# A down projection with tokens on the output partitions

## What is computed

```python
def rmsnorm(x, g):
    y = x * rsqrt(mean(x * x, axis=-1, keepdims=True) + 1e-6)
    return y * g

def conv_gated_mlp(h, w_gate, w_up, conv_ffn_w, conv_ffn_b, w_down):
    g = causal_dwconv(h @ w_gate, conv_ffn_w, conv_ffn_b)     # 2048 -> 6144
    return (gelu(g) * (h @ w_up)) @ w_down                    # 6144 -> 2048

x = x + rmsnorm(hybrid_mixer(rmsnorm(x, norm_mix_pre), ...), norm_mix_post)   # called x1 below
h = rmsnorm(x, norm_ffn_pre)
x = x + rmsnorm(conv_gated_mlp(h, ...), norm_ffn_post)
```

## Time and profile before

| | |
|---|---|
| median of 3 runs | 2304.57 us (2303.58 to 2305.54) |
| the profiled execution | 2304.29 us |
| its span, first to last instruction | 2302.6 us |
| TensorE matmul, busy | 2230.5 us, 97% |
| VectorE, ScalarE, busy | 1559.4 us, 989.0 us |
| mean granted TensorE clock | 0.985 of full speed |
| last matmul of the down projection starts | 2263.23 us |

### The profile page before, as it was taken

How to read it: one execution, slowest core, us unless ns; L and a number is a source line. 1 busy time by engine, 2 the same in 40 slices (tenths; PEclk the granted TensorE clock), 3 DMA queues, 4 the chain that set the end, 5 groups by cost and what they waited for, 6 DMA issues and landing times.

```text
span 2302.6 us, 34618 instructions
## 1 busy us (share of the span) xinstructions
PE 2230.5 (97%) x13324; PEld 1970.7 (86%) x13324; DVE 1559.4 (68%) x2022; ACT 989.0 (43%) x1232; POOL 202.0 (9%) x250
## 2 busy tenths in 40 slices
PE   8999999999899899999999999999999999999993
PEld 6788888888688688999999999999998888888882
DVE  8776667767755677788888888888885454544543
ACT  5444545544422354444444444444443343333431
POOL 3000000003300000111111111111102000000002
PEclk9899999999999999999999999999999999999997
DMA  4222222222242335877777777777767322222224
GB/s 170 68 93 79 90 93 82 93 85 75 95 141 91 114 128 163 216 206 199 206 205 202 199 202 205 204 204 203 207 175 284 125 93 99 93 99 91 100 91 82
DMA packets 94966, 325.15 MB, mean 141 GB/s; under 512 B 10753, under 2 KB 14977, under 8 KB 94737
## 3 DMA queue, kind: packets, MB, share of 16 engines
q1 hardware_dynamic: 68160, 237.18, 30.2%
q0 software_dynamic: 24400, 82.36, 16.9%
q10 hardware_dynamic: 2304, 4.20, 0.5%
HBM read 302.69 MB, written 21.00 MB: 141 GB/s over the span
## 4 chain that ended last, share of the span: by engine, by line
PE 93%; DVE 2%; issue 1%; ACT 1%; POOL 1%; DMA 1%; SPq 0%; DVEq 0%; POOLq 0%; ACTq 0%
PE bank L1447 31%; PE bank L1449 31%; PE bank L1448 30%; PE bank L1509 1%; POOL out L476 1%; DVE acc_b L1102 1%; DMA x_sb<-xT 0%; ACT act_hi L612 0%; DVE w_lo L842 0%; PE bank L1477 0%; DMA h_t<-h_spill 0%; ACT w_hi L486 0%; DVE rms L863 0%; PE bank L1528 0%; ACT act_hi L636 0%
## 5 line engine op out<-in xcount | busy, mean ns | idle before, releaser
L1447 PE MATMUL bank<-act_hi,w_hi 128*128 128x512 f32 (+1 forms) x2880 | 1026.7, 356 | 22.3 <-DVE act_lo L857 13.5
L1449 PE MATMUL bank<-act_hi,w_lo 128*128 128x512 f32 (+1 forms) x2880 | 1019.0, 354 | 0.0
L1448 PE MATMUL bank<-act_lo,w_hi 128*128 128x512 f32 (+1 forms) x2880 | 1013.7, 352 | 0.0
L1447 PEld LDWEIGHTS bank<-act_hi,w_hi 128*128 128x128 f32 x2880 | 545.3, 189 | 103.0 <-DVE w_lo L842 10.9
L1449 PEld LDWEIGHTS bank<-act_hi,w_lo 128*128 128x128 f32 x2880 | 544.9, 189 | 81.1
L1448 PEld LDWEIGHTS bank<-act_lo,w_hi 128*128 128x128 f32 x2880 | 544.9, 189 | 78.2 <-issue 0.7
L1449 PE MATMUL bank<-tsum,w_lo 128*128 128x256 f32 x1344 | 374.1, 278 | 0.0
L1448 PE MATMUL bank<-tsum,w_hi 128*128 128x256 f32 x1344 | 374.1, 278 | 0.0
L1447 PE MATMUL bank<-tsum,w_hi 128*128 128x256 f32 x1344 | 374.0, 278 | 0.0
L852 DVE TENSOR_TENSOR w_lo<-raw,w_hi 128x1024 fp32r<-128x1024 f32 x96 | 117.6, 1225 | 271.1 <-ACT w_hi L492 271.1
L842 DVE TENSOR_TENSOR w_lo<-raw,w_hi 128x1024 fp32r<-128x1024 f32 x138 | 171.9, 1246 | 185.7 <-ACT w_hi L486 183.5
(11 more groups left out here) (222 smaller groups left out, 1811.4 us busy)
## 6 DMA issues: line engine op xcount, KB each, us to landing
raw<-weights SPq DMA_DIRECT2D x318, 512.0 KB, 3.5
raw_s<-weights SPq DMA_DIRECT2D x84, 512.0 KB, 5.0
raw_s<-weights POOLq DMA_DIRECT2D x84, 512.0 KB, 6.1
raw_a<-weights SPq DMA_DIRECT2D x42, 512.0 KB, 5.2
h_spill<-h_out POOLq DMA_DIRECT2D x48, 256.0 KB, 3.7
h_t<-h_spill POOLq DMA_DIRECT2D x24, 512.0 KB, 6.5
x<-xT POOLq DMA_DIRECT2D x16, 256.0 KB, 2.9
out<-x ACTq DMA_DIRECT2D x16, 256.0 KB, 2.1
```

Source lines behind the costliest of these rows:

```text
L1447: pe.matmul(dst, ah, bh, start=start, stop=False, skip_group_check=goes_on)
L1448: pe.matmul(dst, ah, bl, start=False, stop=False, skip_group_check=goes_on)
L1449: return pe.matmul(dst, al, bh, start=False, stop=stop, skip_group_check=goes_on)
```

## The change

The operands of the down projection trade places: the stationary one is a hidden tile's 128 tokens, the moving one 512 output channels of the weights. A bank then holds 128 tokens by 512 channels, and a group gives the same 512 channels as before for all tokens, in four banks of 128 tokens each. From this follows the rest:

- Groups 0 to 2 are copied out of PSUM by VectorE (`tensor_copy`) into `y_tile(i)`, 128 tokens by 2048 channels, and ScalarE squares them with a row sum (`accum_out`) into `y_sq`. The multiplications by `rms` and by the gain and the additions into `acc` are gone.
- The factor `rms` cancels in the norm but for its epsilon, so the norm's epsilon becomes one per token, `eps_y`. It is computed once, in the gate projection: four more matmuls (`column_sum`) in `x1_sum`, one small VectorE instruction, and a wait of TensorE before unit `U_FF+12`.
- In the last unit, for each 128 tokens: ScalarE squares the bank with a row sum, VectorE adds the four sums, ScalarE takes the root of 128x1, VectorE the reciprocal, ScalarE scales the last 512 channels out of PSUM, VectorE the first 1536.
- TensorE transposes the result back, 16 tiles of four 128x128 transposes, through four banks, in the order `LIFTS`. Twelve tiles are taken by VectorE, which multiplies by the gain and adds x1 in one instruction, and SyncE stores them two at a time with plain DMAs. The other four (tiles 0 to 3, `ADDED`) are taken by ScalarE into two buffers, and GpSimd stores them with adding DMAs; tiles 2 and 3 wait until the stores of tiles 0 and 1 have landed.
- x1 for the twelve tiles is read back from `out` (3 MB, one DMA of GpSimd) into `x1_b`, where the first hidden tiles lay, in the last group.

```diff
+ADDED = 4
+LIFTS = (4, 5, 0, 6, 7, 1, 8, 9, 2, 10, 11, 3, 12, 13, 14, 15)
...
+        def h_tokens(t, s, kt, i):
+            c = HS + i % 2 * P
+            return t[:, 4 * s + 2 * kt + i // 2, c:c + P]
...
+            for k in range(0, KT - ADDED, 2):
+                sp.wait_ge(taken, k + 2)
+                sp.dma_start(out[:, ADDED + k:ADDED + k + 2], x1_b[:, k:k + 2]).then_inc(stored, 16)
+            sp.wait_ge(stored, 16 * (KT - ADDED) // 2)
...
             pool.wait_ge(x1_stored, 16 * KT)
-            for k in range(KT):
-                pool.wait_ge(yd_scaled, k + 1)
-                pool.dma_start(out[:, k], yd_tile(k), accum_op=ALU.add).then_inc(stored, 16)
-            pool.wait_ge(stored, 16 * KT)
+            pool.wait_ge(h_split, 3 * PER_GROUP + 6)
+            pool.dma_start(x1_b[:], out[:, ADDED:KT]).then_inc(x1_back_landed, 16)
+            for k in range(ADDED):
+                pool.wait_ge(added, k + 1)
+                pool.dma_start(out[:, k], y_out[:, k % 2], accum_op=ALU.add).then_inc(y_added[k % 2], 16)
+            for e in range(2):
+                pool.wait_ge(y_added[e], 16 * ADDED // 2)
...
             def down_square(g, i):
-                act.wait_ge(wd_taken, 4 * g + i + 1)
-                act.activation(sq[:, 0], sq[:, 1], ACT.Square).then_inc(wdsq_done, 1)
+                if g < GROUPS - 1:
+                    act.wait_ge(wd_taken, QT * g + i + 1)
+                    src = y_tile(i)[:, S * g:S * g + S]
+                else:
+                    act.wait_ge(last_done, i + 1)
+                    src = DOWN_BANKS[g % 2][i][:]
+                act.activation(sq[:, 0], src, ACT.Square, accum_out=y_sq[:, i, g:g + 1]).then_inc(wdsq_done, 1)
...
-            for i in range(4):
-                act.wait_ge(wd_scaled, i + 1)
-                act.activation(sq_last[:, i], yd_tile(KT - 4 + i), ACT.Square).then_inc(wdsq_done, 1)
-            root(6, SUM, std)
+            for i in range(QT):
+                down_square(GROUPS - 1, i)
+                act.wait_ge(y_summed, i + 1)
+                act.activation(y_r[:, 1, i:i + 1], y_r[:, 0, i:i + 1], ACT.Sqrt, scale=1.0 / D,
+                               bias=eps_y[:, i:i + 1]).then_inc(y_std_done, 1)
+                act.wait_ge(y_r_done, i + 1)
+                act.activation(y_tile(i)[:, 3 * S:], DOWN_BANKS[1][i][:], ACT.Copy, scale=y_r[:, 2, i:i + 1]).then_inc(
+                    y_scaled_a, 1)
+            for n, k in enumerate(LIFTS):
+                if k < ADDED:
+                    act.wait_ge(lifted, n + 1)
+                    if k > 1:
+                        act.wait_ge(y_added[k % 2], 16 * (k // 2))
+                    act.activation(y_out[:, k % 2], LIFT[n % 4][:], ACT.Copy, scale=col("g_ffn_post", k)).then_inc(
+                        added, 1)
...
             invert_root(5, rms[:], std, 4)
+            dve.wait_ge(sum_done, 6)
+            dve.tensor_scalar(eps_y[:], PT[2][:, 0:QT], EPS / D, EPS * EPS, ALU.mult, ALU.add).then_inc(eps_y_done, 1)
             chain(dve.memset(gb[:, 0:2], 0.0))
             split(U_FF + 12, 0)
...
             def down_tile(g, i):
-                t = 4 * g + i
-                if i:
-                    add_down_square(t - 1)
-                else:
+                if not i:
                     dve.wait_ge(unit_used, U_HID + (g + 1) * PER_GROUP)
-                dve.tensor_tensor(sq[:, 1], DOWN_BANKS[g % 2][i][:], rms[:], ALU.mult).then_inc(wd_taken, 1)
-                dve.wait_ge(wd_taken, t + 1)
-                dve.tensor_scalar(yd_tile(t), sq[:, 1], col("g_ffn_post", t), None, ALU.mult)
+                dve.tensor_copy(y_tile(i)[:, S * g:S * g + S], DOWN_BANKS[g % 2][i][:]).then_inc(wd_taken, 1)
...
-            for i in range(4):
-                dve.wait_ge(last_done, i + 1)
-                dve.tensor_tensor(yd_tile(KT - 4 + i), DOWN_BANKS[1][i][:], rms[:], ALU.mult).then_inc(wd_scaled, 1)
-                if i:
-                    add_down_square(KT - 4 + i - 1)
-            invert_root(6, rms[:], std, 5)
-
-            dve.wait_ge(wd_scaled, 4)
-            for k in range(KT):
-                if k < KT - 4:
-                    dve.tensor_tensor(yd_tile(k), yd_tile(k), rms[:], ALU.mult).then_inc(yd_scaled, 1)
-                else:
-                    dve.scalar_tensor_tensor(out=yd_tile(k), in0=yd_tile(k), scalar=col("g_ffn_post", k), in1=rms[:],
-                                             op0=ALU.mult, op1=ALU.mult).then_inc(yd_scaled, 1)
+            for i in range(QT):
+                dve.wait_ge(wdsq_done, QT * (GROUPS - 1) + i + 1)
+                dve.tensor_reduce(y_r[:, 0, i:i + 1], y_sq[:, i], AXX, ALU.add).then_inc(y_summed, 1)
+                dve.wait_ge(y_std_done, i + 1)
+                dve.reciprocal(y_r[:, 2, i:i + 1], y_r[:, 1, i:i + 1]).then_inc(y_r_done, 1)
+                dve.wait_ge(y_r_done, i + 1)
+                dve.tensor_scalar(y_tile(i)[:, 0:3 * S], y_tile(i)[:, 0:3 * S], y_r[:, 2, i:i + 1], None,
+                                  ALU.mult).then_inc(y_scaled_d, 1)
+            dve.wait_ge(x1_back_landed, 16)
+            for n, k in enumerate(LIFTS):
+                if k >= ADDED:
+                    dve.wait_ge(lifted, n + 1)
+                    dve.scalar_tensor_tensor(out=x1_b[:, k - ADDED], in0=LIFT[n % 4][:], scalar=col("g_ffn_post", k),
+                                             in1=x1_b[:, k - ADDED], op0=ALU.mult, op1=ALU.add).then_inc(taken, 1)
...
                 channel_sum(SB[2], acc[:])
+                column_sum(PT[2], acc)
...
             tile(U_FF + 10, PJ[1], between=x1_sum)
+            pe.wait_ge(eps_y_done, 1)
             tile(U_FF + 12, PT[2])
...
                 for kt in range(2):
+                    w = slice(S * kt, S * kt + S)
                     for i, bank in enumerate(out_banks):
-                        last = product(halves(bank[:]), w_tile(s, 4 * kt + i),
-                                       (h_half(act_hi, s, kt), h_half(act_lo, s, kt)),
-                                       start and kt == 0, stop and kt == 1)
+                        last = product(bank[:], (h_tokens(act_hi, s, kt, i), h_tokens(act_lo, s, kt, i)),
+                                       (w_hi[:, s, w], w_lo[:, s, w]), start and kt == 0, stop and kt == 1)
...
-            pe.wait_ge(wdsum_ready, 1)
-            pe.matmul(SUM[:], ones[:], acc[:], start=True, stop=False)
-            pe.wait_ge(wdsq_done, KT)
-            pe.matmul(SUM[:], ones[:], sq_last[:, 3], start=False, stop=True).then_inc(sum_done, 1)
+            for n, k in enumerate(LIFTS):
+                if n >= 4:
+                    before = LIFTS[:n - 3]
+                    at_least(pe, taken, sum(b >= ADDED for b in before))
+                    at_least(pe, added, sum(b < ADDED for b in before))
+                if k == 12:
+                    pe.wait_ge(y_scaled_a, QT)
+                for i in range(QT):
+                    if n == 0:
+                        pe.wait_ge(y_scaled_d, i + 1)
+                    last = pe.transpose(LIFT[n % 4][:, P * i:P * i + P], y_tile(i)[:, P * k:P * k + P], ident[:])
+                last.then_inc(lifted, 1)
```

More of the change, by code:

```diff
@@ L150, in block_kernel @@
         cols = sb("cols", [2, QT])
+        eps_y = sb("eps_y", [QT])
+        y_sq = sb("y_sq", [QT, GROUPS])
+        y_r = sb("y_r", [3, QT])
         banks = [ctx.enter_context(nc.psum_tensor(f"bank{i}", [P, S], F32)) for i in range(8)]
@@ L153, in block_kernel @@
         DOWN_BANKS = (banks[0:4], banks[4:8])
-        SUM = banks[0]
+        LIFT = banks[0:4]
         region_a = ExitStack()
@@ L162, in block_kernel @@
         sb("act_hi_first", [KT // 2, S])
-        yd_a = sb("yd_a", [KT // 2, S])
+        y_a = sb("y_a", [2, D])
         sb("act_lo_first", [KT // 2, S])
-        yd_b = sb("yd_b", [KT // 2, S])
+        y_b = sb("y_b", [2, D])
         mix = ExitStack()
@@ L237, in block_kernel @@
         h_t = sb_in(hid, "h_t", [FT, S])
-        sq_last = sb_in(hid, "sq_last", [4, S])
+        y_out = sb_in(hid, "y_out", [2, S])
         hid.close()
+        fin = ExitStack()
+        x1_b = sb_in(fin, "x1_b", [KT - ADDED, S])
+        fin.close()
         names = """par_landed hi_done split_done unit_used consts_set zeros_set
@@ L252, in block_kernel @@
             a11_landed a12_landed a22_landed s3_half s3_landed s2_done s4_done
-            p1_copied pu_done pw_done c22_done c11_taken c12_done c12_taken c21_done wd_scaled last_done
-            wd_taken wdsq_done wdsum_ready diag_done spread_done yd_scaled
+            p1_copied pu_done pw_done c22_done c11_taken c12_done c12_taken c21_done last_done
+            wd_taken wdsq_done y_summed y_std_done y_r_done y_scaled_a y_scaled_d diag_done spread_done eps_y_done
+            x1_back_landed lifted added taken
             stored dve_chain""".split()
@@ L268, in block_kernel @@
          a11_landed, a12_landed, a22_landed, s3_half, s3_landed, s2_done, s4_done,
```

(21 more changed lines are left out.)

5 lines of the change are left out of this document (removed).

## The result

The changed kernel takes 2337.91 us at the median (2336.42 to 2338.63), the kernel before 2305.06 on the same chip: a ratio of 1.0142, with a 95% interval of 1.0125 to 1.016. It is 33 us slower, where 10.6 us less were forecast.

A forecast was written before the change was run, and what follows sets the result against it. TensorE bounds the down projection, so the gain had to come from the 39.0 us end, bound by DMA engines while stores run. End at 2291.0 plus 1.0 gives 2292.0 against 2302.6, -10.6 us: forecast 2294.0, range 2288 to 2301.

The forecast's parts named there:

- The matmuls: Down projection: moving operand as one run of 512 in place of two of 256, 0.2286 us either way, cost nothing.
- Rival (c): Down projection: traded operands raise matmul pitch; gain gone at +4.6 ns, slower at +6.6 ns, time 2309.2 us; chance 0.06.
- The column sums: Gate projection: four fp32 matmuls in TensorE's queue cost their whole length, +1.0 us, bounds 0.5 and 1.3.
- Reading x1 back: Last group: 3.1 MB beside the weight loads costs nothing; if a load were held up, a stall of 3.2 us, once.
- No ScalarE wait: Last group: a sign expected in the profile after, that ScalarE does not wait for a weight load.
- The norm: Last unit: four rounds of 2.15 us, one table load of 1.28, scaling done 6.1 us behind the last matmul.
- The clock of the lifts: End: TensorE's transposes back run at half clock, 0.86 us a tile, the last at 2283.1.
- rival (a): End: full clock for the lifts, 0.44 us a tile, time 2291.0 us; chance 0.18.
- The stores: End: DMA work of 14.4 us against 24.7, a lone adding store landing in 4.0, closing 5.0, end at 2291.0.
- rival (b): End: stores share DMA engines badly, tiles 2 and 3 wait for 0 and 1; time 2301.0 at 8 us landings; chance 0.15.

The follow-up runs named there:

- the experiment with the pad alone: Kernel before, with 160 unused bytes a partition allocated behind cols and nothing else changed: 2348.11 us, ratio 1.0187.
- one pair of kernels: Kernel before and changed kernel, each with eps and cols (changed: also its three small tensors) ahead of raw, distance 0: 2324.23 and 2313.61 us.
- the other: Kernel before with 64 bytes ahead of w_hi2, 2289.61 us; changed kernel with that, small tensors away and hidden halves 64 bytes lower, 2273.06 us.

## Why the prediction was wrong

**The matmuls: wrong, and decisive.** The step that failed is "0.2286 us either way. Cost nothing." That put the change of the matmuls' pitch at nothing; the runs show +44 us from the shifted tensors and +10 from the traded operands. The step had compared the form of the moving operand (one run or two) in the earlier trace rows, and left out where the operands lie: both stages had the distance 64, so the rows could not show it. Two parts of the change move that. The three small tensors shift everything behind them by 160 bytes, which costs 44 us over the whole kernel (2348.11 - 2304.46 in the experiment with the pad alone). And trading places turns the distance of 64 in the down projection into -64, which costs 10 us by itself. With the small tensors in the way too, the two don't add: the distance there is then -224, or 32, which is on the same slow level. I had also taken the rest of the kernel as untouched because its code was; a tensor's size is part of the code of every stage.

**Rival (c)** had the right sign, the right place and nearly the price for one part (+4.4 ns, 10.2 us, where it said +4.6 for a lost gain), with the wrong reason: other engines' writes. It got 0.06. That the forecast is wrong if the pitch moves stood among its signs, but the pitch was looked for in the down projection alone.

**The column sums: right.** Forecast +1.0 us. TensorE in the changed kernel:

```profile
858.86 0.95 PE L1514 MATMUL bank<-ones,acc 128*128 128x1 f32 x8
859.67 0.48 PE L1478 MATMUL bank<-act_hi,w_hi 128*128 128x512 f32 x1
```

From 858.86 to 859.67 they hold the queue, for 0.81 us.

**Reading x1 back: right in cost, wrong in cover.** TensorE never stood still for it, but it took 12.8 us to land, and the weight load beside it 9.4, where I had 7.5 at most against a slack of 8.5. ScalarE waited for that load. The chain of waits of the changed kernel (us in total, times, longest), and the window of that stretch:

```profile
ACT w_hi L516 <- DMA raw<-weights: 4.4, 1, 4.4
```

```profile
2200.00:2220.00 20.00, 20.00 (x88) 16.05 (x87) 7.22 (x7) 7.26 (x8) 0.55 (x1) 1.00 0.68 260
```

TensorE is busy for 20.00 of 20.00 us all the same. The splits start every 5.60 us (2201.97, 2207.57), and the one that waited for the load starts at 2213.96, only 0.8 us behind that beat: for the rest of the 4.4 us it would have waited for TensorE to free the slot. "No ScalarE wait" was the wrong sign to look for.

**The norm: right.** Round 1's square starts 2.02 us ahead of round 2's (forecast 2.15), one table load, and the last scaling ends 5.4 us after the last matmul (forecast 6.1). The row sum ended at 2304.86, the table load started at 2304.88 and the root at 2306.17, so this trace has no room for the drain that the Trainium skill (ScalarE: Activation LUTs, What ACT_TABLE_LOAD costs) puts beside a load.

**The clock of the lifts: half right.** The windows of the changed kernel; the column behind POOL is the clock, then DMA share and GB/s:

```profile
2308.00:2312.00 4.00, 0.97 (x5) 0.36 (x3) 2.68 (x6) 3.12 (x8) 0.00 (x0) 1.00 0.00 0
...
2314.00:2316.00 2.00, 2.00 (x10) 2.00 (x11) 1.50 (x2) 0.00 (x0) 0.00 (x0) 0.50 0.03 8
...
2317.00:2318.00 1.00, 1.00 (x10) 1.00 (x9) 1.00 (x2) 0.00 (x0) 0.91 (x1) 0.87 1.00 406
2318.00:2320.00 2.00, 2.00 (x20) 2.00 (x19) 1.88 (x4) 0.69 (x1) 0.89 (x1) 1.00 0.87 108
```

The clock fell after nearly idle microseconds, as forecast, and the first transposes ran at 0.50: two start every 0.43 us, 0.86 for a tile. But from about 2317 it was back at full speed, with nothing but transposes on TensorE since 2313.82. Its timeline on both sides of that point:

```profile
2315.80 0.63 PE L1785 MATMUL bank<-ident,y_a 128*128 128x128 f32 x2
2316.22 0.64 PE L1785 MATMUL bank<-ident,y_b 128*128 128x128 f32 x2
...
2318.04 0.38 PE L1785 MATMUL bank<-ident,y_b 128*128 128x128 f32 x2
2318.26 0.38 PE L1785 MATMUL bank<-ident,y_a 128*128 128x128 f32 x2
```

Two in 0.22 us are 0.44 for a tile, the price of rival (a), 0.18. The forecast held for the first 3 us and rival (a) for the rest. What the Trainium skill says of transposes and the clock (TensorE: Matmul & The Clock Gate, PE-mode transpose), and by which the half clock would have lasted to the end, doesn't hold in this trace: the clock rose from 0.50 to 1.00 under transposes alone.

**The stores: right in total.** The DMA queues of the changed kernel from 2313 to 2336, 23 us, and the landings of the adding stores (line 499):

```profile
q1 hardware_dynamic: 864, 3.15, 34.5%
q0 software_dynamic: 576, 1.05, 31.0%
```

```profile
DMA to landing us min/median/max: 4.2/6.2/7.4
```

65.5% of 23 us are 15.1 us of all engines, where 14.4 were forecast. The landings took longer than the 4.0 that I gave them, and ScalarE waited 2.6 and 3.3 us for the buffers of tiles 2 and 3 (the brackets in the first section's timeline). This is rival (b)'s wait, there but small, and four buffers, which take it away, gained nothing that the runs can tell. The early return of the clock and the longer landings worked against each other: 28.4 us from the last matmul's end, with 27.4 forecast. That the total came so near is in part luck.

So the sum of what the change computes was right in size: at equal distances it is worth 10.6 us by one pair of kernels and 11.5 by the other. The sum lacked a term of +44 for where the tensors lie, which doesn't belong to anything that the change computes.

## What to carry to other kernels

A few bytes of new tensors shift every operand that is allocated behind them, and swapping the operands of a matmul turns the sign of their distance. Here the first cost four times what the edit gained, and the second about all of it. Busy time and clock show none of it: take the starts of two matmuls, or their count in a window, in a stage that the diff doesn't touch, and compare them before looking for a cause in the new code. When two versions are compared, pad them so that the operands have the same distances; then try the distance itself. Here 64 bytes in one place were worth 0.6% to the old kernel, and two such places 1.3% to the changed one (2302.72 to 2273.06): distance 0 modulo 256 bytes for 512 columns, 64 to either side for this kernel's 256-column stage. Work out the distance with its sign, from the addresses of both.

## What the runs showed of the hardware that I had not expected

- The pitch of a stream of fp32r matmuls whose operands start at multiples of 32 bytes depends on the moving operand's start less the stationary one's, modulo 256 bytes. With 512 columns: 0.2267 us at 0, 0.2292 at +64, 0.2333 to 0.2344 at the other multiples of 32, -64 among them. With 256 columns, in the kernels: 0.1133 at 64 and at -64, 0.1196 to 0.1200 at 0, 0.1184 at 224.
- At distance 0 with both operands 16 or 4 bytes off a multiple of 32 it was 0.2333 and 0.2375 with 512 columns.
- The same offsets gave 0.114 or 0.118 us with 256 columns in two kernels; what else decides stayed open.
- The granted clock went from 0.50 (2316 to 2317) to 1.00 (2318 to 2320) while TensorE did nothing but transposes.
- A table load stood between the end of the row sum and the root with 0.02 us ahead of it and 0.01 behind.
- Adding stores took 31.0% of 23 us for 1.05 MB (6.8 us per MB) beside plain ones at 34.5% for 3.15 MB (2.5 us per MB), and a store of 256 KB that adds landed in 6.2 us at the median, where one of 512 KB that doesn't took 5.2.
